# Two transformer blocks on one core: the order of work on ScalarE and VectorE in the first attention

## The reference

```
# 8 sliding-window heads: softmax over 256 keys with a sink in the sum
s = jnp.einsum('bnqgrd,bnkgd->bngrqk', qb, kb) * scale - slope * dist   # masked
m = jnp.maximum(jnp.max(s, -1), sg);  e = jnp.exp(s - m)
o = (e / (jnp.sum(e, -1) + jnp.exp(sg - m))) @ vb
# 8 NSA heads, 3 branches each: compressed keys ("cmp"), selected ("sl"), window ("wn")
p = softmax(q @ k.T * scale - slope * dist)
o = gate_c * (p_c @ v_cmp) + gate_s * (p_s @ v_slc) + gate_w * (p_w @ v_win)
x = x + rmsnorm(concat([o_nsa, o_swa]) @ w_o)
```

## Time and profile before

| | |
|---|---|
| median of 3 runs | 1281.78 us (1281.46 to 1284.89) |
| the profiled execution | 1282.99 us |
| its span in the trace | 1281.1 us |
| TensorE busy | 1263.2 us |
| VectorE, ScalarE, GpSimd busy | 786.1, 648.3, 219.3 us |
| granted TensorE clock, mean | 0.999 |
| the steps of the first attention | 72 to 233 us of the span |

### The profile page before, as it was taken

How to read it: one execution, slowest core, us unless ns; L and a number is a source line. 1 busy time by engine, 2 the same in 40 slices (tenths; PEclk the granted TensorE clock), 3 DMA queues, 4 the chain that set the end, 5 groups by cost and what they waited for, 6 DMA issues and landing times.

```text
span 1281.1 us, 16451 instructions
## 1 busy us (share of the span) xinstructions
PE 1263.2 (99%) x6004; PEld 1044.4 (82%) x6004; DVE 786.1 (61%) x1465; ACT 648.3 (51%) x1261; POOL 219.3 (17%) x234
## 2 busy tenths in 40 slices
PE   9999999999999999999999999999999999999998
PEld 8888888878888888888787777887888888888887
DVE  6779877686545565356888877588644343343334
ACT  6688777554344433233545645486633252332344
POOL 0066655001100010001002101032311030110111
PEclk9999999999999999999999999999999999999999
DMA  7311111423333333332423212432333324243332
GB/s 271 91 50 42 34 33 41 164 83 107 98 93 98 99 91 99 99 91 66 121 86 99 83 56 68 126 116 64 99 99 99 92 76 121 75 115 91 99 89 67
DMA packets 64625, 118.20 MB, mean 92 GB/s; under 512 B 7712, under 2 KB 12192, under 8 KB 64288
## 3 DMA queue, kind: packets, MB, share of 16 engines
q1 hardware_dynamic: 62704, 112.86, 29.5%
q10 hardware_dynamic: 1840, 4.29, 1.1%
HBM read 115.02 MB, written 2.10 MB: 91 GB/s over the span
## 4 chain that ended last, share of the span: by engine, by line
PE 89%; DVE 5%; issue 2%; POOL 1%; ACT 1%; DMA 1%; SPq 0%; POOLq 0%; ACTq 0%; DVEq 0%
PE bank L594 25%; PE bank L596 25%; PE bank L595 25%; PE bank L695 2%; PE bank L696 2%; PE bank L694 2%; PE bank L814 2%; PE bank L800 1%; POOL pp L2983 1%; PE bank L801 1%; PE bank L827 1%; PE bank L828 1%; DVE ptl L2221 1%; DVE q2p L2205 1%; DMA raw<-in_w_ple 1%
## 5 line engine op out<-in xcount | busy, mean ns | idle before, releaser
L2036 DVE TENSOR_TENSOR wl<-raw,wh 128x512 fp32r<-128x512 f32 (+2 forms) x360 | 267.8, 755 | 326.9 <-ACT wh L1332 326.3
L1332 ACT ACTIVATE wh<-raw 128x512 fp32r<-128x512 f32 (+1 forms) x398 | 242.8, 620 | 285.1 <-PE bank L596 273.0
L594 PE MATMUL bank<-AH,wh 128*128 128x512 f32 (+1 forms) x848 | 331.3, 391 | 2.1 <-DVE AL L2050 0.8
L596 PE MATMUL bank<-AH,wl 128*128 128x512 f32 (+1 forms) x848 | 329.4, 388 | 0.0
L595 PE MATMUL bank<-AL,wh 128*128 128x512 f32 (+1 forms) x848 | 327.6, 386 | 0.0
L594 PE MATMUL bank<-BH,wh 128*128 128x512 f32 x624 | 246.8, 396 | 0.0
L596 PE MATMUL bank<-BH,wl 128*128 128x512 f32 x624 | 244.9, 392 | 0.0
L595 PE MATMUL bank<-BL,wh 128*128 128x512 f32 x624 | 243.6, 390 | 0.0
L594 PEld LDWEIGHTS bank<-AH,wh 128*128 128x128 f32 x848 | 159.4, 188 | 36.7 <-issue 2.9
L596 PEld LDWEIGHTS bank<-AH,wl 128*128 128x128 f32 x848 | 159.3, 188 | 33.6
L595 PEld LDWEIGHTS bank<-AL,wh 128*128 128x128 f32 x848 | 159.3, 188 | 33.5 <-issue 0.2
(11 more groups left out here) (356 smaller groups left out, 1625.2 us busy)
## 6 DMA issues: line engine op xcount, KB each, us to landing
raw<-in_w_dn SPq DMA_DIRECT2D x104, 256.0 KB, 2.7
raw<-in_w_gu SPq DMA_DIRECT2D x88, 256.0 KB, 2.6
raw<-in_w_up SPq DMA_DIRECT2D x64, 256.0 KB, 2.6
raw<-in_w_nsa SPq DMA_DIRECT2D x16, 256.0 KB, 2.7
raw<-in_w_pg SPq DMA_DIRECT2D x16, 256.0 KB, 2.6
raw<-in_w_naq SPq DMA_DIRECT2D x16, 256.0 KB, 2.6
nbi<-in_na_bias ACTq DMA_DIRECT2D x8, 448.0 KB, 3.4
raw<-in_w_swa SPq DMA_DIRECT2D x10, 256.0 KB, 2.6
```

The lines of the kernel that those rows point to most:

```text
L594: t.matmul(o, w, xh, start=start, stop=False, skip_group_check=skip)
L596: return t.matmul(o, wl, xh, start=False, stop=stop, skip_group_check=skip)
L1332: a.activation(W[i % NW].h[:, 0:n], RAW[i % NRAW][:, 0:n], ACT.Copy).then_inc(*s_wh.up(i))
L2036: v.tensor_tensor(w.l[:, 0:n], RAW[i % NRAW][:, 0:n], w.h[:, 0:n], ALU.subtract).then_inc(*s_wl.up(i))
```

## The change

Nothing is computed otherwise, and no instruction is added or removed but through its place. Four things move within the loops of ScalarE and VectorE; both loops get one more step at their end.

- **ScalarE**: `out_part(u)` goes from the end of step u+3 to step u+4, behind the exponentials of that step; `out_high` goes one step later. The high halves of the keys ("k") go from ahead of the step's exponentials to behind them, still ahead of `out_part`.
- **VectorE**: the step's order was soft, vc, out_add(s-4), out_low(s-5), rest1(s-3), norm1(s-1). It becomes soft, rest1(s-3), out_low(s-6), vc, norm1(s-1), out_add(s-4).
- **VectorE**: the low halves of the keys go one step later, one group behind soft, the other at the end of the step behind `out_add`.
- **VectorE**: for wide units from u = 10 the reciprocal (`inverse1`) goes to the head of step u+1, ahead of `soft1(u+1)`. It waits for the exponentials of unit u.

```diff
@@ -1545,11 +1545,14 @@
                     return
                 elif n == 1 and key[0] == "q":
                     queries(key[1])
-                elif n == 1:
+
+            def filled_keys(name, i):
+                key, n = fill_info(name, i)
+                if n == 1 and key[0] == "k":
                     keys_of(key[1], KS1[key[1]])
 
             later = []
-            for s in range(N_UNITS + 4):
+            for s in range(N_UNITS + 5):
                 for name, i in later:
                     filled(name, i)
                 if s < N_UNITS:
@@ -1565,11 +1568,18 @@
                         if kind == "swa":
                             m = a.activation(G4[s % 6], M4[s % 6], ACT.Exp, bias=sink[:, j + 4 * g:j + 4 * g + 1])
                         m.then_inc(*s_ex.up(s))
+                for name, i in later:
+                    filled_keys(name, i)
                 if s == 0:
                     hidden(0)
                     hidden(1)
                 if s == 2:
                     comp_keys()
+                if 4 <= s < N_UNITS + 4 and closes(s - 4):
+                    key = out_key(s - 4)
+                    n = key[2] + (0 if key[1] == "swa" else 4)
+                    out_part(key, key[3], out_sum(key), s_pv.at(s - 4),
+                             *([s_xl.at(("ob", "swa", n - 2) if n < 6 else ("ob", "nsa", n - 6))] if n >= 2 else []))
                 for name, i in FILL1.get(s, ()):
                     if name == "w_o_swa":
                         evicted(i)
@@ -1591,13 +1601,8 @@
                         for r in (0, 64):
                             m = a.activation(VC[g][r + 32 * g:r + 32 * g + 31, half(0)], bank.ap(("vc",))[x, 0:64], ACT.Copy)
                     m.then_inc(*s_qh.up("vc"))
-                if 3 <= s < N_UNITS + 3 and closes(s - 3):
-                    key = out_key(s - 3)
-                    n = key[2] + (0 if key[1] == "swa" else 4)
-                    out_part(key, key[3], out_sum(key), s_pv.at(s - 3),
-                             *([s_xl.at(("ob", "swa", n - 2) if n < 6 else ("ob", "nsa", n - 6))] if n >= 2 else []))
-                if s >= 4 and closes(s - 4) and unit(s - 4)[2] == 1:
-                    pair = out_key(s - 4)[0:3]
+                if s >= 5 and closes(s - 5) and unit(s - 5)[2] == 1:
+                    pair = out_key(s - 5)[0:3]
                     out_high(pair, out_sum(pair), out_pair(pair), s_xl.at(("x0", 7)) if pair[1] == "swa" else s_cm.at(("hid", 1)))
                 later = FILL1.get(s, ())
 
@@ -2267,7 +2272,6 @@
 
             def norm1(u):
                 kind, j, g = unit(u)
-                s4 = S4[u % 6]
                 if kind == "cmp":
                     s8 = S8.rearrange(pairs8, g=2)
                     e.wait_ge(s_ex.at(u))
@@ -2278,12 +2282,17 @@
                     v.tensor_tensor(s8, s8, gate_of(u), ALU.mult).then_inc(*s_nm.up(("g", u)))
                     e.wait_ge(s_nm.at(("g", u)))
                     v.tensor_tensor(p3, p3, s8.unsqueeze(3).broadcast_to([P, 2, 4, 31]), ALU.mult).then_inc(*s_nm.up(u))
-                else:
-                    e.wait_ge(s_ex.at(u))
-                    if kind == "swa":
-                        v.tensor_tensor(s4, s4, G4[u % 6], ALU.add).then_inc(*s_nm.up(("s", u)))
-                        e.wait_ge(s_nm.at(("s", u)))
-                    v.reciprocal(s4, s4).then_inc(*s_nm.up(("r", u)))
+                elif u < 10:
+                    inverse1(u)
+
+            def inverse1(u):
+                kind, j, g = unit(u)
+                s4 = S4[u % 6]
+                e.wait_ge(s_ex.at(u))
+                if kind == "swa":
+                    v.tensor_tensor(s4, s4, G4[u % 6], ALU.add).then_inc(*s_nm.up(("s", u)))
+                    e.wait_ge(s_nm.at(("s", u)))
+                v.reciprocal(s4, s4).then_inc(*s_nm.up(("r", u)))
 
             def rest1(u):
                 kind, j, g = unit(u)
@@ -2307,18 +2316,29 @@
                 key, n = fill_info(name, i)
                 if n == 1 and key[0] == "q":
                     queries_low(key[1])
-                elif n == 1 and key[0] == "k":
-                    for g in range(2):
+
+            def keys_low(parts, g):
+                for name, i in parts:
+                    key, n = fill_info(name, i)
+                    if n == 1 and key[0] == "k":
                         doubled(key, g, tmp.ap(key), T, KS1[key[1]][g])
 
-            later = []
-            for s in range(N_UNITS + 4):
+            earlier, later = [], []
+            for s in range(N_UNITS + 5):
                 for name, i in later:
                     behind(name, i)
                 for name, i in later:
                     filled(name, i)
+                if 10 < s <= N_UNITS and unit(s - 1)[0] != "cmp":
+                    inverse1(s - 1)
                 if s < N_UNITS:
                     soft1(s)
+                keys_low(earlier, 0)
+                if 3 <= s <= N_UNITS + 2:
+                    rest1(s - 3)
+                if s >= 6 and closes(s - 6) and unit(s - 6)[2] == 1:
+                    pair = out_key(s - 6)[0:3]
+                    out_low(pair, out_sum(pair), out_pair(pair))
                 if s == 8:
                     e.wait_ge(s_qh.at("vc"))
                     for g in range(2):
@@ -2328,28 +2348,24 @@
                                                 VC[g][x, half(0)], ALU.subtract)
                     m.then_inc(*s_ql.up("vc"))
                     bank.read(("vc",), (s_ql, "vc"))
+                if 1 <= s <= N_UNITS:
+                    norm1(s - 1)
+                if s == 3:
+
+                    g3 = gates[:, :].rearrange("p (b h k) -> p b h k", b=4, h=8)[:, :, :, 0]
+                    e.wait_ge(s_fn.at(("gates", 3)))
+                    v.tensor_tensor(g3, g3, rowv.unsqueeze(2).broadcast_to([P, 4, 8]), ALU.mult).then_inc(*s_dv.up("gv"))
                 if s >= 4 and closes(s - 4):
                     key = out_key(s - 4)
                     out_add(key, key[3], out_sum(key))
-                if s >= 5 and closes(s - 5) and unit(s - 5)[2] == 1:
-                    pair = out_key(s - 5)[0:3]
-                    out_low(pair, out_sum(pair), out_pair(pair))
-                if 3 <= s <= N_UNITS + 2:
-                    rest1(s - 3)
-                if 1 <= s <= N_UNITS:
-                    norm1(s - 1)
-                if s == 3:
-
-                    g3 = gates[:, :].rearrange("p (b h k) -> p b h k", b=4, h=8)[:, :, :, 0]
-                    e.wait_ge(s_fn.at(("gates", 3)))
-                    v.tensor_tensor(g3, g3, rowv.unsqueeze(2).broadcast_to([P, 4, 8]), ALU.mult).then_inc(*s_dv.up("gv"))
+                keys_low(earlier, 1)
                 for name, i in later:
                     filled_low(name, i)
                 if s == 2:
                     for g in range(2):
                         e.wait_ge(s_z.at("zero"))
                         doubled(("k", "c"), g, tmp.ap(("k", "c")), 31, KC1[g])
-                later = FILL1.get(s, ())
+                earlier, later = later, FILL1.get(s, ())
             out_low(("ob", "nsa", 3), OS[1], B[3])
 
             def y1(c):
```

More of the change, by code:

```diff
@@ L2330, in vector @@
                     bank.read(("vc",), (s_ql, "vc"))
-                if s >= 4 and closes(s - 4):
-                    key = out_key(s - 4)
-                    out_add(key, key[3], out_sum(key))
-                if s >= 5 and closes(s - 5) and unit(s - 5)[2] == 1:
-                    pair = out_key(s - 5)[0:3]
-                    out_low(pair, out_sum(pair), out_pair(pair))
-                if 3 <= s <= N_UNITS + 2:
-                    rest1(s - 3)
                 if 1 <= s <= N_UNITS:
@@ L2345, in vector @@
                     v.tensor_tensor(g3, g3, rowv.unsqueeze(2).broadcast_to([P, 4, 8]), ALU.mult).then_inc(*s_dv.up("gv"))
+                if s >= 4 and closes(s - 4):
+                    key = out_key(s - 4)
+                    out_add(key, key[3], out_sum(key))
+                keys_low(earlier, 1)
                 for name, i in later:
```

## The result

The kernel before takes 1281.78 us, the changed one 1300.49 us (median of 4 runs, 1298.89 to 1302.09): a ratio of 1.0134, 95% interval [1.012, 1.0149], 18.7 us slower. The forecast was 1290.6, with a range from 1283.5 to 1296. The sign and the main mechanism (the loop through both engines) were as predicted; the size, 18.7 us, is over twice the 8.8 us of the forecast.

What follows compares the result with a forecast made beforehand. TensorE, busy 1263.2 of 1281.1 us, was taken as the bound. Step terms 10.5 - 0.6 + 0.6 + 0 - 0.3 - 1.4 gave +8.8 us, taking 1281.78 to 1290.6 us; range 1283.5 to 1296.

Steps and rivals of the forecast that it cites:

- the loop through both engines: Closing attention steps: soft, exponentials, out_part, out_add, next soft form a chain, 5.0 us (swa) or 5.4 (NSA) bare.
- The signs: Attention waits: out_add's wait for out_part 20 us or more, singles about 4; TensorE idle at L827, L814, L867, two fills.
- Steps 7 and 8: Step 7: soft(7) at 106.5, +0.6 us; step 8: vc behind soft(8) and rest1(5), 3.2 us of wait, +2.4 net.
- Steps 9 and 10: Step 9: an old TensorE wait goes, -0.4 us; step 10: fill waits for out_add(5), then soft(10), +1.1.
- Steps 11 and 12: Step 11: L867 2.4 us behind the scores, plus small waits, +3.4 us; step 12: fill waits for soft(12)'s bank, +1.4.
- Steps 13 and 14: Attention steps 13 and 14: 2.2 us of old waits go, L867 of step 14 waits 1.5 for out_add(10): -0.6 us.
- Steps 15 to 17, 18 to 20, 23 to 25: Later attention: +0.6 us as VectorE is just behind; 0 as 0.9 of old waits offsets lag and a fill wait; -0.3.
- Steps 27 to 29: Last attention steps, where no soft and no bank of a join hangs on the wait: -1.4 us.
- The lock between VectorE and GpSimd: Attention: GpSimd's divisions would be quicker and the keys' low halves collide, up to 0.9 us either way, slack over 3.
- Covered: Rival, attention: TensorE's steps cover the join's wait, only removed waits count, -4 to -6 us, 1276.8 us; chance 0.06.
- half and half: Rival, attention: swa steps lose 4 to 6 us, NSA steps win 3 to 5, giving 1282.5 us; chance 0.13.
- The third: Rival, NSA steps: the loop bounds them too, each round loses 2 us more, some 15 us, 1296.5 us; chance 0.16.

Runs made afterwards that it cites:

- e1_join_back: Changed kernel with ScalarE's out_part back at the end of step u+3, ahead of the next exponentials, VectorE's order kept as changed: 1283.38 us, ratio 1.0003 to the kernel before.
- e6b_awake: Changed kernel with 20 extra matmuls of 256 columns on TensorE ahead of the last scores of step 11, products overwritten: 1299.34 us, ratio 1.0124 to the kernel before.
- e7_lows_ahead: Changed kernel with VectorE's low halves of the queries and second group of the keys' low halves ahead of out_add: 1290.85 us, ratio 1.0059 to the kernel before.
- e4_recip_only: Kernel before with only the reciprocals of wide units from u = 10 moved to the head of VectorE's next step: 1282.58 us, ratio 0.9992.
- e2_vc_first: Changed kernel with VectorE's four instructions for the compressed values (vc) ahead of keys and rest1 in step 8: 1300.85 us, ratio 1.0134 to the kernel before.
- e3_keys_back: Changed kernel with the high and low halves of the keys back at their old places on both engines: 1300.47 us, ratio 1.0135 to the kernel before.

## Why the prediction was wrong

Point by point, with its own steps. What TensorE lost in each is the difference between its lateness at the start of that step's transposes and at the start of the next step's (the next step's fill lies between), from the table above and the same two timelines.

- **The loop exists and costs** (right). e1_join_back shows it by taking it away. `out_add(0)` waited 3.3 us, until 92.37, and soft(5) started at 92.98 (predicted: 91.9 and 92.6); soft(6) at 100.33 (99.9). The hand-over, estimated at 0.05 us, is 0.03 from the end of ScalarE's copy to the start of `out_add`. The signs came: up to 240 us `out_add` waits 17.9 us (20 or more forecast), the longest wait is 3.3 (about 4), and TensorE waits at L827, in step 8, at L867 twice and in front of both fills.
- **Steps 5 and 6**: +1.3 and +0.7 predicted, 1.3 and 0.8 measured. Right. All the lateness in the table has 0.5 us from ahead of the changed part (it is there at step 2), which no step of the sum had.
- **Steps 7 and 8**: +3.0 together, 3.3 measured, but this is two misses that cancel: step 7 lost 1.7 us (0.6 predicted), step 8 1.7 (2.4). Soft(7) started at 107.97, not at 106.5, so the lateness came a step earlier; the wait for vc was put at 3.2 and is 2.6. Soft(8) was taken as 2 us and took 1.8 (113.72 to 115.54), not the 3 of the earlier trace rows; that choice was right.
- **Steps 9 and 10**: +0.7 predicted, 1.2 measured. Step 10's fill waits 1.7 us instead of 1.1.
- **Steps 11 and 12**: +4.8 predicted, 8.0 measured. This is the largest miss. L867 is as predicted (2.45 idle against 2.4) and the fill cost 1.2 in starts (1.4). The transposes and scores of step 11 wait more than was put down for them: 1.06 and 0.25 us of idle time for soft(11), 1.8 in starts, and up to L867 step 11 lost 4.4 instead of 3.4. The step that failed is that a late matmul was priced at its lateness alone: TensorE stood 3.4 us almost without a break (140.5 to 144.4), the granted clock was 0.50 from 143.5 on, and the fill's 12 matmuls took 5.3 us instead of 2.9 (131.63 to 134.51 in before), which is 2.4 us. The ledger had no term for it. That the standing brings it is borne out for this place by four traces, three with the wait and the spell and e6b_awake with neither.
- **Steps 13 and 14**: -0.6 predicted, +0.2 measured. L867 of step 14 waits 1.39 us (predicted 1.5), but the starts slip by more than the idle time, and the gain from old waits was put too high (0.9 us in step 13; 2.2 forecast for both).
- **Steps 15 to 17, 18 to 20, 23 to 25**: predicted +0.6, 0 and -0.3, measured 1.7, 0.7 and 0.5. **Steps 27 to 29**: -1.4 predicted, -0.9 measured (at L867 of step 29 it is 17.4 us late, 239.09 against 221.72). Together 3.1 us too low. Most of the first is one wait: step 17's fill stands 1.51 us (until 176.64) for soft(17), behind an `out_add` that waits 2.26 us and two low halves of 2.38; in e7_lows_ahead these steps lose nothing. "VectorE is just behind" was put at 0.6. The gain from early reciprocals came, but not whole: of the 2.7 us of waits for divisions 0.4 is left, and the reciprocal has its own price on soft and `ptl` (e4_recip_only: 2.7 gone, 2.3 come). Nor does it free a division that stands behind a low half of a weight in GpSimd's queue. VectorE and GpSimd of after in step 28:

```profile
233.16 0.18 DVE L2295 RECIPROCAL small<-small 128x4 f32<-128x4 f32 x1 [0.83 <-ACT pp L1518]
...
234.21 1.28 POOL L2973 TENSOR_TENSOR wl<-raw,wh 128x512 fp32r<-128x512 f32 x1 [1.93 <-ACT wh L1332]
235.48 2.81 POOL L2999 TENSOR_SCALAR pp<-pp,small,gates 128x128 f32<-128x128 f32 x4
```

  The sums are ready at 233.3, the division starts at 235.5, and TensorE waits for it at 238.35 after all. The prediction moved the reciprocal past VectorE's queue and didn't ask what is ahead of the division on GpSimd's.
- **The lock between VectorE and GpSimd** was weighed as "up to 0.9 us either way" beside a slack of 3 us, "and the sum stays". Here is its place in step 6, VectorE, then GpSimd:

```profile
104.75 0.68 DVE L2233 TENSOR_TENSOR os<-bank,os 64x512 f32<-64x512 f32 x1 [1.50 <-ACT os L1529]
105.47 2.47 DVE L2128 TENSOR_TENSOR qs<-tmp,qs 64x512 fp32r<-64x512 f32 x2
107.97 0.35 DVE L2210 CUSTOM_DVE_ANT_0 pp<-bank,ds,small 128x128 f32<-128x128 f32 x1
...
105.37 1.30 POOL L2973 TENSOR_TENSOR wl<-raw,wh 128x512 fp32r<-128x512 f32 x1
```

  The two low halves take 2.47 us instead of the 1.50 of the earlier trace rows, with soft(7) right behind them. The same happens in step 10 (2.46 us at 134.94), and to the cmp unit's last product in step 9 (1.38 us at 125.41, over GpSimd's 1.32 at 125.20, instead of 0.42) and to the low halves of step 16 (2.38 us for two at 173.26). Each is about 1 us inside a loop without slack, just ahead of the steps 7, 10, 11 and 17 in which TensorE was later than in the ledger; I read them as its cause there, which no run shows by itself. What was wrong isn't the 0.9 but the sentence on slack: that of GpSimd was counted, and the instruction that is held up was VectorE's, in the loop. The Trainium skill's rule (SBUF — State Buffer, "SBUF: two separate sides": the loser of the lock is held for the other's instruction) agrees for GpSimd's operations with two SBUF inputs, by these rows. The other part of that paragraph came out: from step 6 on the four divisions took 2.05 to 2.81 us in after and 2.07 to 3.93 in before. In e7_lows_ahead the pair of step 6 ran beside divisions instead (1.54 us at 102.84), and those of steps 10 and 16 (1.55 and 1.40 us) had no GpSimd operation with two SBUF inputs in front either; how much of its 9.6 us is the lock and how much the place in the queue wasn't separated.
- **Behind the attention**: 0 predicted, 1.7 in the profile. TensorE doesn't wait more there; it is 17.6 us late up to 778 us and 19.1 behind 782, and its mean granted clock is 0.72 from 776 to 782 us of after, in a stretch in which it is busy throughout, right behind 16 matmuls of one column. e2_vc_first has the same spell at the same matmuls (0.72, too); the profiles of e1_join_back, e3_keys_back, e6b_awake and e7_lows_ahead have nothing like it there. So it isn't this one execution's alone, and what brings it stays open.
- **The rivals.** "Covered" and "half and half" fell. The third, that the NSA steps lose too, is closer in size: from step 12's transposes to the end of the attention the kernel lost 2.2 us where -1.7 was forecast. But its mechanism, 2 us lost in every round, isn't seen: from one cmp step to the next (15, 20, 25, end) TensorE loses 2.4 and 0.5 us and wins 0.9.

The misses in one sum: 8.8 forecast, + 0.5 ahead, + 0.9 in steps 5 to 10, + 3.2 in 11 and 12 (2.4 of it clock, 1.0 the waits of step 11, less 0.2 at the fill), + 3.9 from 13 to 29, + 1.7 behind; together 19.0, against 19.1, the difference of the spans. So some 4 us of the 10 missing are clock, and most of the rest is VectorE's lag behind the loop, put too small in steps 11 and 15 to 17. The range was too narrow upward because all its bounds were durations; none was for the clock or for a term of gains that fails. (The forecast's own range was added up loosely, too: its bounds give 1286.1 to 1293.6, not 1285.6 to 1293.5.)

## What to carry to other kernels

When a step is moved behind a wait, write down the closed path through both engines, then put nothing between the waiting instruction and the one that the loop needs next: work that nobody awaits goes ahead of the wait (9.6 us here, for the order of a few instructions). A producer's copy belongs a step ahead of its consumer, and a ready input frees an instruction only if its own queue is empty: look at what stands ahead of it there. A loss that leaves TensorE standing for two or three microseconds at a time can be larger than the standing, as the clock may fall behind it (2.4 us here); a forecast of a slower kernel wants a term for that.

## What the hardware showed

- Granted clock 0.50 for 6.8 us (143.5 to 150.3 in after), beginning within 3.4 us of nearly unbroken standing (140.5 to 144.4); in it the fill's 12 matmuls took 5.3 us instead of 2.9. In e7_lows_ahead a stretch at 0.50 comes with a wait of 3.1 us. First the fill that waited, then a stretch of the same kernel:

```profile
126.05 0.79 PE L594 MATMUL bank<-AH,wh 128*128 128x512 f32 x1 [3.09 <-DVE os L2233]
126.64 0.63 PE L595 MATMUL bank<-AL,wh 128*128 128x512 f32 x1
...
126.00:129.00 3.00, 2.95 (x7) 2.37 (x8) 2.98 (x11) 1.81 (x3) 0.00 (x0) 0.50 0.00 0
```

  In the traces of after and of the experiments each of the 15 stretches at 0.50 inside the attention begins during a wait of TensorE of 1.4 to 4.6 us or at most 1.9 us behind one. The reverse doesn't hold: the wait for vc of 2.6 us in step 8 has such a stretch behind it in e3_keys_back (118.5) and e6b_awake (117.4) and none in after. Outside the attention after and e2_vc_first have one at 778 us with no wait ahead of it. What decides between these no run here shows.
- A VectorE operation with two SBUF inputs (64x512) that starts 0.1 to 0.2 us behind a GpSimd one with two (128x512, 1.3 us) takes some 1 us more than alone (1.67 to 1.75 us instead of 0.69), as in the rows of step 6 above. Beside GpSimd's divisions (one tile input) the same operation took 0.68 to 0.94 us in after.
